# Dense units of a decoder step: token half outermost, so that 24 matmuls in a row add into one PSUM bank

## The reference, cut to what matters

```python
m = silu(c) @ w_ada + b_ada                    # shift, scale and gate of three sub-layers
h = x + 0.5 * gate1 * swiglu1(mod1(rms_norm(x)))
u = mod2(rms_norm(h)); p = u @ w_in            # q, k, v, gates, short convolution, merge gates
A = nsa(...) @ w_nsa_out
Bc = (B * conv3(C * h_cv)) @ w_conv_out
h = h + gate2 * ((sig(gA) * A + sig(gB) * Bc) @ w_out)
h = h + 0.5 * gate3 * swiglu2(mod3(rms_norm(h)))
y = rms_norm_final(h)
```

## Time and profile before

| | |
|---|---|
| time of three runs | 1551.17, 1551.66, 1552.94 us; median 1551.66 us |
| span of the profiled execution | 1549.8 us, 27898 instructions (it has no other time) |
| TensorE busy | 1457.5 us, 94%, 11238 matmuls and 11238 weight loads |
| VectorE busy | 559.9 us, 36% |
| ScalarE busy | 468.7 us, 30% |
| GpSimd busy | 117.3 us, 8% |
| mean granted TensorE clock | 0.972 |

### The profile page before, as it was taken

How to read it: one execution, slowest core, us unless ns; L and a number is a source line. 1 busy time by engine, 2 the same in 40 slices (tenths; PEclk the granted TensorE clock), 3 DMA queues, 4 the chain that set the end, 5 groups by cost and what they waited for, 6 DMA issues and landing times.

```text
span 1549.8 us, 27898 instructions
## 1 busy us (share of the span) xinstructions
PE 1457.5 (94%) x11238; PEld 1328.3 (86%) x11238; DVE 559.9 (36%) x1156; ACT 468.7 (30%) x755; POOL 117.3 (8%) x128
## 2 busy tenths in 40 slices
PE   7997999999999997999979989989879999999996
PEld 5676999999999987999979735449879999999995
DVE  0105333333233235335323365746352323332334
ACT  0115332323211124121222355553253434331211
POOL 0402000000001112000000000004320000000110
PEclk9998999999999998999999999999989999999998
DMA  9893444444423341332273423313313232222321
GB/s 343 295 359 109 145 153 150 148 154 144 151 80 84 84 108 52 84 94 76 82 115 116 139 80 91 94 42 112 93 41 95 81 94 82 88 71 77 93 83 66
DMA packets 83540, 180.20 MB, mean 116 GB/s; under 512 B 18341, under 2 KB 43429, under 8 KB 81742
## 3 DMA queue, kind: packets, MB, share of 16 engines
q1 hardware_dynamic: 83470, 179.23, 37.3%
HBM read 173.07 MB, written 10.28 MB: 118 GB/s over the span
## 4 chain that ended last, share of the span: by engine, by line
PE 88%; DVE 4%; ACT 3%; DMA 3%; issue 1%; SPq 1%; ACTq 0%; DVEq 0%
PE PS L1419 71%; PE PS L1342 3%; PE PS L1634 3%; PE PS L1610 3%; DMA raw<-in_w_in 2%; PE PS L1440 2%; PE PS L1623 2%; DVE rinv L943 1%; PE PS L1446 1%; PE PS L1323 1%; ACT uh L710 1%; DMA ada<-in_w_ada 1%; ACT tmp L714 1%; SPq L425 1%; PE PS L1392 0%
## 5 line engine op out<-in xcount | busy, mean ns | idle before, releaser
L1419 PE MATMUL PS<-uh,wh 128*128 128x272 f32 x2032 | 429.3, 293 | 36.4 <-DVE ul L961 26.9
L936 DVE TENSOR_TENSOR wl<-raw,wh 128x1024 fp32r<-128x1024 f32 (+2 forms) x215 | 239.8, 1116 | 587.6 <-ACT wh L685 587.4
L685 ACT ACTIVATE wh<-raw 128x1024 fp32r<-128x1024 f32 (+2 forms) x215 | 203.6, 948 | 815.7 <-PE PS L1419 800.6
L1419 PE MATMUL PS<-uh,wl 128*128 128x272 f32 x2032 | 422.6, 290 | 0.0
L1419 PE MATMUL PS<-ul,wh 128*128 128x272 f32 x2032 | 422.1, 289 | 0.0
L1419 PEld LDWEIGHTS PS<-uh,wh 128*128 128x128 f32 x2032 | 320.9, 190 | 40.0 <-issue 37.3
L1419 PEld LDWEIGHTS PS<-ul,wh 128*128 128x128 f32 x2032 | 322.3, 190 | 0.0
L1419 PEld LDWEIGHTS PS<-uh,wl 128*128 128x128 f32 x2032 | 320.5, 191 | 0.0
L1419 PE MATMUL PS<-hh,wh 128*128 128x272 f32 x704 | 145.7, 288 | 0.9 <-DVE tmp L1010 0.9
L1419 PE MATMUL PS<-hh,wl 128*128 128x272 f32 x704 | 145.7, 288 | 0.0
L1419 PE MATMUL PS<-hl,wh 128*128 128x272 f32 x704 | 145.1, 288 | 0.0
(11 more groups left out here) (224 smaller groups left out, 1281.4 us busy)
## 6 DMA issues: line engine op xcount, KB each, us to landing
raw<-in_w_gu SPq DMA_DIRECT2D x88, 512.0 KB, 3.7
ada_t<-in_w_ada_t SPq DMA_DIRECT2D x44, 512.0 KB, 4.3
raw<-in_w_in SPq DMA_DIRECT2D x39, 512.0 KB, 3.7
ada<-in_w_ada SPq DMA_DIRECT2D x7, 2048.0 KB, 9.7
raw<-in_w_dn SPq DMA_DIRECT2D x32, 384.0 KB, 3.2
raw<-in_w_dn SPq DMA_DIRECT2D x32, 320.0 KB, 2.9
ch<-in_cmp_pages SPq DMA_DIRECT2D x64, 128.0 KB, 3.9
kv<-in_sel_pages SPq DMA_DIRECT2D x128, 64.0 KB, 1.9
```

What stands on the lines that cost most here:

```text
L685: e.activation(wh[:, u % SPLITS, 0:n, :], raw[:, u % RAWS, 0:n, :], ACT.Copy).then_inc(hi_ready, 1)
L936: e.tensor_tensor(wl[:, u % SPLITS, 0:n, :], raw[:, u % RAWS, 0:n, :], f(wh[:, u % SPLITS, 0:n, :]), ALU.subtract).then_inc(lo_ready, 1)
L1419: ins = mm(o[:, a, :], w[:, u % SPLITS, k, :], x[:, k0 + k, HT * a:HT * a + HT], start=(first and k == 0 and w is wh and x is xh), stop=(l ...
```

## The change

Inside `unit`, the loop over the two token halves `a` moves from innermost to outermost. A unit first does all blocks of k and all three products for half 0, in the first bank of its pair, then all for half 1, in the second. The waits for `ready` are kept in the pass over half 0 alone. Number, operands and shapes of the matmuls stay; the start flag falls on the first matmul of each half, as before, and the stop flag on the last of each half. The signal `unit_used` stays on the unit's last matmul.

```diff
@@ -1411,11 +1411,11 @@
                 n = unit_k(u)
                 o = out2(slot)
                 e.wait_ge(lo_ready, u + 1 + more)
-                for k in range(n):
-                    if ready is not None:
-                        e.wait_ge(ready[0], ready[1] + k0 + k + 1)
-                    for w, x in ((wh, xh), (wh, xl), (wl, xh)):
-                        for a in range(2):
+                for a in range(2):
+                    for k in range(n):
+                        if ready is not None and a == 0:
+                            e.wait_ge(ready[0], ready[1] + k0 + k + 1)
+                        for w, x in ((wh, xh), (wh, xl), (wl, xh)):
                             ins = mm(o[:, a, :], w[:, u % SPLITS, k, :], x[:, k0 + k, HT * a:HT * a + HT],
                                      start=(first and k == 0 and w is wh and x is xh),
                                      stop=(last and k == n - 1 and w is wl))
```

## The result

The changed kernel takes **1576.55 us** (median of 4 runs, 1576.28 to 1577.18), the kernel before in the same comparison 1551.70 us (1551.17 to 1552.94). The ratio is 1.0157, interval 1.0145 to 1.0169: slower by 24.9 us. The forecast was 1569, with a range of 1559 to 1576; the time lies just above its high end.

The account below looks back on a forecast made before the run. The prediction took the kernel as bound by 8976 successive matmuls at 125 ns. Pace 0, waits 10.5 and clock 7.5 made 18.0 us on the span of 1549.8, 1567.8; with 1.9 for the median, it said 1569, range 1559 to 1576.

Parts of the forecast that it names:

- What stays: Whole kernel: same matmuls, loads, waits, signals and DMA; evacuation and buffers keep their place; cost zero if the pace holds.
- The cover that I gave as 0.8 us: Conv unit: the last conv low part ends at 738.63 and is now wanted at 739.47, leaving 0.8 us.
- Step 1: Dense matmuls: successive ones in one bank keep the pace of 125 ns; taken as 0 us.
- signs of being wrong: Anywhere: a dense pace off by over 0.5 ns, or a stage with no first unit that changed its length.
- 3 ns drawn from L1342: Longer matmuls of L1342: an excess of 3 ns, against 11.7 ns over streaming in the dense stretch.
- rival C: Dense matmuls: one bank costs 1 ns each, 9 us more, 1579 us; chance 0.10.
- Step 2: Four first units with inputs still arriving: 27 matmuls in place of 6 after the last delivery, 2.63 us each, 10.5 in all.
- Step 3: Same four first units: the 27 matmuls begin at half clock; 2.1 us at three, 1.2 at the output projection, 7.5 in all.
- 876.5 row: Clock window 876.5 to 879 of the kernel before: TensorE busy 1.48 of 2.50 us, clock stayed at 0.50.
- A: First units: waits cost 10.5 us but the clock rises as before, 1562 us; chance 0.16.
- B: Dense matmuls: faster, as alternating banks partly lift the pace from 113 to 125 ns; 1465 or 1544 us; chance 0.06.
- D: Whole kernel: no effect, input waits hidden or cancelled by a 2 ns gain of pace, 1552 us; chance 0.06.

Follow-up runs that it names:

- one-bank run: Kernel before, old loop order, both halves adding into the first bank except at the last block of k: 1552.73 us against 1552.57, ratio 1.0001.
- filled kernel: Changed kernel plus three discarded matmuls after each of the first 7 blocks in waiting 8-block units: 1567.58 us against 1552.57 for the kernel before.
- input-units kernel: Kernel before, with the half outermost only in units that wait for inputs per k: 1569.70 us against 1552.57, ratio 1.0111.
- changed kernel with one input half: Changed kernel, both passes reading the columns of half 0, half 1 left out: 1578.73 us against 1551.29 for the kernel before, ratio 1.0176.
- snake: Kernel before, with the middle product taking half 1 first, so halves go 0 1 1 0 0 1: 1548.75 us against 1548.16, ratio 1.0002.
- bank-every-third run: Kernel before, for each k three products of half 0, then three of half 1: 1558.01 us against 1550.94, ratio 1.0049.

## Where the prediction was right, and the step that failed

**What stays** held: same instructions, and no new gap in the down projections, the merge units or the attention stage (its difference is -0.02 us). (The seven units that the prediction says wait per k are seven places, with thirteen such units; that changes nothing, since the same four count.) The cover that I gave as 0.8 us for the last conv part sufficed.

**Step 1 failed.** I put the pace's term at 0 and allowed up to 0.5 ns in the forecast, from rows of other matmuls. It measured 5.8 us: 0.5 ns in the FFN loops, 0.2 in the down loops, 1.1 to 1.2 in the written-out projections. Two of the prediction's own signs of being wrong came true: a dense pace off by over 0.5 ns, and stages without a first unit that changed their length. The conclusion about the bank was right, and the one-bank run confirms it (806 matmuls in both windows), where the 3 ns drawn from L1342 had hung on two cycles a column, which no run here tests. The conclusion about the pace was wrong, since I took the bank for the only thing that the order changes. The order also sets which input columns follow each other, and no row of before with another order of these existed; that these columns can move the pace is shown, by what mechanism, and what else acts beside them, stays open. The bound of 1 ns that I named was of the right size, and I left it out of the range by calling it rival C. The advice of the Trainium skill (Perfetto Trace Analysis, section Matmul Optimizations) to use all 8 PSUM banks for more parallelism would have been a reason for a loss of pace; the one-bank run shows none from the bank, 1.0001.

**Step 2 was right,** to the tenth: 2.63 us a unit was forecast, and with the clock held up the filled kernel shows 2.65, 2.63 and 2.62 us at the norm-fed units.

**Step 3 was right** in kind, and in size to 1 us. The 876.5 row was a fair witness: the clock of a TensorE with 1.48 us of work in 2.50 did not rise from 0.50, and neither did it in the first units. Forecast for the clock were 7.5 us over four places, measured 16.95 - 10.5 = 6.5, too much at three and too little at one: at the norm-fed units 4.33, 3.94 and 4.34 less 2.63 are 1.7, 1.3 and 1.7, where I said 2.1; at the output projection 1.7, where I said 1.2. Both steps together: 18.0 forecast, 16.95 measured. With three matmuls per delivery the clock had not risen when the last input came; with six, in the kernel before and in the filler kernel, it had. The Trainium skill (TensorE: Matmul & The Clock Gate, Part 1) says that activity releases the clock, and the trace agrees for the gapless stretches from 606 on and of the filler kernel.

**What no step had:** 2.55 us at half clock, at the start of the down projection and in the norm ahead of FFN 2. The first fall also stands in the profiles of the input-units kernel (+1.55) and of the changed kernel with one input half, but not in that of the filler kernel, which has the changed loops everywhere; and it stands in that of the snake (+1.53), whose waits are those of the kernel before. So the change is not needed for it. But it stands in all three profiles of kernels with the changed first units and no filler, and in one of the ten others, so the change probably makes it likelier; with one profile of each, that is not shown. The slow norm matmuls stand in the kernel before too, at another norm. Pace 5.8 plus 2.55 less 0.58 of a sooner start, less 1.05 in steps 2 and 3, is the 6.7 us by which the span missed the forecast; the median missed the stated 1569 by 7.55, since 1569.7 was rounded down and the median stands 2.05 us above the span after, 1.86 before.

**Rivals.** A (waits without clock, 1562) is refuted by the windows and by the filler run. B (faster by bank) is refuted by the one-bank run: with the waits of before it gained nothing. No order tried came below 124.39 ns on the mean of the written-out units, where the kernel before has 124.50. C (one bank costs 1 ns, 1579) had the time nearly right and the reason wrong: a pace loss did come, 0.65 ns on the mean of 8976 matmuls (5.8 us), and not from the bank. D is refuted by every first unit.

## What to carry to other kernels

When a loop is turned inside out, look first at the unit whose inputs are still arriving: what stands behind the last delivery (here 27 matmuls in place of 6) is pure loss, and if the engine idles between deliveries, it also meets that work at half clock. Where that cannot be avoided, order the unit so that as little as possible needs the last input; that alone beat the tuned kernel by 0.15% (0.04 to 0.26). And do not price an order of matmuls by its banks alone: changing only which input columns are read cost up to 1.6 ns a matmul, so such a change wants one profile of a dense stretch, where counting matmuls in 100 us tells it at once. Count in more than one stage: the snake lost 1.7 ns in one projection and nothing in the next.

## What was not expected of the hardware

- The pace of a stream of loads and matmuls depends on which input columns are read: in the written-out projections 124.5 ns with halves alternating, 126.1 with both from half 0, 125.6 in the changed order. The loops react by 0.1 to 0.8 ns, in other proportions. It does not depend on them alone: the snake order gave 126.1 in the input projection and 124.5 in merge gates that read the same tensors, and down loops in the old order ran at 125.03 in one kernel and 125.27 in another. Why is open; an effect of where inputs or instructions lie in memory was not tried.
- Accumulating 42 successive matmuls into one bank in the old order costs nothing: ratio 1.0001 (0.9992 to 1.0011). With 24 in a row, half and product outermost, the written-out projections still ran at 124.39 ns.
- Executions of one kernel differ by chance, in more places than one. The granted clock of the span goes with its time: of the 31 runs of the kernel before beside the bank-every-third run, the three at 0.971 had 1552.9 us on the mean and the four at 0.975 had 1549.8. And the load ahead of the merge, 25.30 us on the chain before, took 22.12 in the snake's profile; in the input-units kernel the same stage was 3.45 us longer, and that profiled execution, 1574.19 us, is the slowest of its four. Single profiles can so differ by 3 us for no reason of the edit; where they were compared here, it was stage by stage.
- Discarded matmuls made the changed kernel some 9 us faster; 6.5 us of it came from a clock at 1.00 for the work behind the last input.
